# Squares of six RMS norms summed on GpSimd ahead of the ones-product on TensorE

## The chip, the cores and the metric

The kernel runs on one core of a Trainium2 chip. The metric is the device time of one execution in microseconds. The time before is the median of three runs; one further execution was profiled, and all rows are from that one.

## What is computed

The reference is a forward pass over 512 tokens of width 1024 in fp32. It has three layers: an RWKV-7 time mix, an attention layer with low-rank queries and keys (MLA), and a layer with windowed attention beside multiscale pooling. Each is followed by a feed-forward block (width 2816). What matters here is the norm that stands before and behind most of these parts:

```
def rmsnorm(x, g):
    xf = x.astype(jnp.float32)
    y = xf * lax.rsqrt(jnp.mean(xf * xf, axis=-1, keepdims=True) + NORM_EPS)
    return (y * g.astype(jnp.float32)).astype(x.dtype)

x = x + rmsnorm(m, norm_g[layer, 1])                       # behind a mixer's output product
f = conv_ffn(rmsnorm(x, norm_g[layer, 2]), ...)
x = x + rmsnorm(f, norm_g[layer, 3])                       # behind the feed-forward's output product
```

## The kernel before

**Layout.** Activations lie transposed: features on the 128 partitions, the 512 tokens along the free axis, so a width of 1024 is 8 tiles of 128x512 (`x`, `m`). A norm's mean runs over features, thus over partitions and tiles.

**The sum of squares.** For tile j, ScalarE squares a tile into `sq[(first + j) % 2]` (`square`, L559; two buffers in turn). TensorE multiplies the 128x128 constant `ones` with that buffer and adds the result up in PSUM bank 7 over all tiles (`sum_squares`, L1715). This puts the sum over partitions on every partition. ScalarE takes the root into `std` (`root_mean`, L566) and VectorE the reciprocal into `rstd` (L1005). Operands of this product are plain fp32. Each call leaves two records in the trace. The other products here run on operands split in two (`hi` and `lo`, type fp32r).

**Dense stages.** `dense` (L1696) works through units. A unit is one output tile of 128 features by 512 tokens, in bank `r` = unit mod 4. For each of its k tiles it issues three products (`w_hi` with `hi`, `w_lo` with `hi`, `w_hi` with `lo`). `w_o`, `o_w` and `out` have 8 units of 8 k tiles. The last part of each feed-forward's output product (`f0dn2`, `f1dn2`, `f2dn2`) has 8 units of 6 k tiles. With `norm_of` set, the sum of squares j is issued behind unit j + 1, and the last one behind sum 6 at the end of the stage. These six stages feed the norms `n_wo`, `n_f0out`, `n_ow`, `n_f1out`, `n_f2` and `n_final`. The other seven norms (`n_mix`, `n_f0`, `n_mla`, `n_ckv`, `n_cq`, `n_f1`, `n_in`) run elsewhere.

**Weights.** SyncE's queue loads a unit's weights into `w_raw[r]` when its last content has been split. ScalarE copies it rounded into `w_hi[r]` (`high`, L553), VectorE subtracts for `w_lo[r]` (`low`, L999). Both work two units ahead of TensorE (`LEAD = 2`). In ScalarE's queue the copy for unit u + 2 stands before the square of tile u (`over_units`, `square_units`).

**Read-out.** Behind a unit, ScalarE (`w_o`, `o_w`, L774 for `w_o`) or VectorE (L1411 in the `dn` stages, L1664 in `out`) takes the bank to SBUF; the square of that tile follows.

**GpSimd** runs one loop in the RWKV part (L544, masks for the triangular inverse) and nothing afterwards. **gconv** is a 128x512 buffer that the feed-forward's gating uses, and (as `gates[1]`) the gated merge before `out`; no dense stage with a norm behind it uses it.

**Semaphores.** `sq_ready` counts squares, `sq_used` the products of all but a norm's last tile, `sum_ready` the last ones, `std_ready` roots. Square j (from j = 2) waits until product j - 2 has used its buffer.

Of the kernel before, what the change touches and what calls it, by code (L numbers as in the profile page):

```python
# [22 lines left out]
ALU = mybir.AluOpType  # L23
# [117 lines left out]
NORM_AT = {}  # L141
_first = 0
for _i, (_name, _n) in enumerate([("n_mix", 8), ("n_wo", 8), ("n_f0", 8), ("n_f0out", 8), ("n_mla", 8), ("n_ckv", 2),
# [2 lines left out]
    NORM_AT[_name] = (_i, _first, _n)  # L146
    _first += _n

NORMED_AT, _first = {}, 0
for _name, _n in (("f0", 8), ("kv", 8), ("q", 8), ("ckv", 2), ("cq", 3), ("f1", 8), ("in", 8), ("f2", 8)):  # L150
    NORMED_AT[_name] = (_first, _n)
# [3 lines left out]
SCALED_AT, _first = {}, 0  # L155
# [86 lines left out]
def build(nc, dram, out_d):  # L242
    with ExitStack() as ctx:
# [7 lines left out]
        def at(name, shape, offset, dt=F32):  # L251
            return nc.alloc_sbuf_tensor_at(name, list(shape), dt, offset=offset)
# [19 lines left out]
        sq = [at(f"sq{i}", [P, T], SQ0 + ROW * i) for i in range(2)]  # L272
# [6 lines left out]
        G1 = place(ROW)  # L279
        gpad, gconv = at("gpad", [P, T + 2], G0), at("gconv", [P, T], G1)  # L280
        gact = sq

        def const(name, rows=slice(0, P), lo=0, hi=None):
            a, n = CONST[name] if name in CONST else LATE[name]
            return (consts if name in CONST else late)[rows, a + lo:a + (n if hi is None else hi)]
# [81 lines left out]
        bank = [ctx.enter_context(nc.psum_tensor(f"bank{b}", [P, T], F32)) for b in range(8)]  # L367

        def signals(text):
            return [ctx.enter_context(nc.semaphore(n)) for n in text.split()]  # L370
# [3 lines left out]
            for n in ("w_loaded", "w_high", "w_split", "unit_done", "bank_free"))  # L374
        (const_loaded, x_loaded, x_back, sq_ready, sq_used, sum_ready, std_ready, rstd_ready, omu_ready) = signals(
            "const_loaded x_loaded x_back sq_ready sq_used sum_ready std_ready rstd_ready omu_ready")
        (resid_tmp, x_ready, normed_tmp, normed_high, normed_low, h_ready, out_ready, out_stored) = signals(
            "resid_tmp x_ready normed_tmp normed_high normed_low h_ready out_ready out_stored")
        (mix_base, mix_tmp, mix_high, mix_low, zeroed) = signals(
# [155 lines left out]
        def _(pool):  # L535
            for j in range(DT):
                for lv in range(1, LEVELS + 1):
                    for p in range(2):
# [4 lines left out]
                        mask = const("level", lo=lv * HEAD, hi=(lv + 1) * HEAD).unsqueeze(1).broadcast_to([P, TT, HEAD])  # L543
                        pool.tensor_tensor(off[p][:, :, :], ab[p][:, :, :], mask, ALU.mult).then_inc(off_ready, 1)  # L544


        @block.scalar
        def _(act):
# [5 lines left out]

            def square(name, source, j):
                i, first, n = NORM_AT[name]
                if j >= 2:
                    act.wait_ge(sq_used, first - i + j - 1)
                act.activation(sq[(first + j) % 2][:, :], source(j), ACT.Square).then_inc(sq_ready, 1)  # L559

            def root_mean(name):
# [7 lines left out]
            def norm(name, source, ready):  # L569

                for j in range(NORM_AT[name][2]):
                    ready(j)
                    square(name, source, j)
                root_mean(name)
# [7 lines left out]
            def late_norm(name, tag, ready):  # L582

                for j in range(DT):
                    ready(j)
                    gained(tag, j)
                    square(name, lambda j: x[:, j, :], j)
                root_mean(name)

            def square_units(phase, name, source, read=None, tag=None):  # L590

                def body(i, r, c):
                    if read is not None:
                        act.wait_ge(unit_done[r], c + 1)
                        read(i, r).then_inc(bank_free[r], 1)
                    act.wait_ge(bank_free[r], c + 1)
                    square(name, source, SLOTS * i + r)
                    if tag is not None:
                        gained(tag, SLOTS * i + r)
                over_units(act, phase, body, high)  # L600
                root_mean(name)
# [275 lines left out]
            for g in range(8 * PAIRS):  # L877
                i, t = g // 8, g % 8
# [81 lines left out]
            for g in range(STEPS2):  # L960
                j, t = g // 8, g % 8
# [716 lines left out]
        def _(pe):  # L1678
            def dense(name, operand, ready=None, then=None, norm_of=None, norm_in=None, inside=None):

                def body(i, r, c):
                    hi, lo = operand(r)
                    kt = KS[name][r]
                    pe.wait_ge(w_split[r], c + 1)
                    pe.wait_ge(bank_free[r], c)
                    for k in range(kt):
                        if norm_in is not None and isinstance(i, int) and i == 0 and r == 0:
                            sum_squares(norm_in, k)  # L1690
                        if inside is not None and isinstance(i, int) and i == 0:
                            inside(r, k)
                        if ready is not None and (r == 0 or name == "lora"):
                            ready(r, k)
                        for n, (w, a) in enumerate(((w_hi, hi), (w_lo, hi), (w_hi, lo))):
                            mm = pe.matmul(bank[r][:, :], w[r][:, k, :], a[:, k, :],  # L1696
                                           start=(k == 0 and n == 0), stop=(k == kt - 1 and n == 2))
                    mm.then_inc(unit_done[r], 1)
                    if then is not None:
                        then(i, r)  # L1700
                    if norm_of is not None and SLOTS * i + r:
                        sum_squares(norm_of, SLOTS * i + r - 1)
                if norm_of is None:
                    over_units(pe, name, body, peel=int(norm_in is not None or inside is not None))
                else:
                    for u in range(UNITS[name]):
                        body(u // SLOTS, u % SLOTS, START[name][u % SLOTS] + u // SLOTS)
                    sum_squares(norm_of, UNITS[name] - 1)

            def sum_squares(name, j):  # L1710
                i, first, n = NORM_AT[name]
                if i and j == 0:
                    pe.wait_ge(std_ready, i)
                pe.wait_ge(sq_ready, first + j + 1)
                mm = pe.matmul(bank[7][:, :], const("ones"), sq[(first + j) % 2][:, :], start=(j == 0),  # L1715
                               stop=(j == n - 1))
                mm.then_inc(sum_ready if j == n - 1 else sq_used, 1)

            def norm(name):
                for j in range(NORM_AT[name][2]):  # L1720
# [7 lines left out]
            for phase in ("r", "k"):  # L1728
                q, _, src = MIXES[phase]
# [342 lines left out]
            for g in range(8 * PAIRS):  # L2072
                i, t = g // 8, g % 8
# [3 lines left out]
                before = FILL_FIRST + 8 * i + sum(n for at_t, n in FILL_BLOCKS.items() if at_t < t)  # L2077
# [90 lines left out]
            for g in range(STEPS2):  # L2168
                j, t = g // 8, g % 8
# [162 lines left out]
```

## Time and profile before

| | us |
|---|---|
| median of 3 runs | 2396.14 (2391.94 to 2396.9) |
| the profiled execution's own time | 2399.1 |
| its span, first to last instruction | 2397.2 |
| TensorE busy (matmul) | 2229.6 (93%) |
| VectorE busy | 1300.2 (54%) |
| ScalarE busy | 929.4 (39%) |
| GpSimd busy | 60.7 (3%) |
| L1715, sums of squares: 93 calls, 186 records | 104.2 busy |
| mean granted TensorE clock | 0.968 of full |

Busy time is an average over stages with different limits. What an instruction in a dense stage costs is read from the chain of work that ended last. Each of its pieces gives the start, the length and the engine and line of work that nothing else covered. PE is TensorE, DVE VectorE, ACT ScalarE, POOL GpSimd. The clock row gives the granted TensorE clock in tenths of full speed (9 stands for 90% and more).

### The profile page before, as it was taken

The numbers are of one execution on the slowest core, as the hardware profiler recorded it, in microseconds if no ns is written. First come the engines' busy times: TensorE is split into PE (matmuls) and PEld (weight loads), VectorE is DVE, ScalarE is ACT, GpSimd is POOL, SyncE is SP. The second block draws the span as 40 slices with busy tenths as digits, with TensorE's granted clock in tenths as the row PEclk, the third lists the DMA queues.
The fourth block names the chain that finished last, engine by engine and source line by source line (L and its number), as shares of the span: only waits on it lengthen the run. The fifth ranks groups of instructions, "written<-read, shape, count | busy, mean of one in ns | idle before, by whom it ended". The sixth has DMA issues, their size and how long they took to land.

```text
span 2397.2 us, 37444 instructions
## 1 busy us (share of the span) xinstructions
PE 2229.6 (93%) x14890; PEld 1728.5 (72%) x14890; DVE 1300.2 (54%) x1978; ACT 929.4 (39%) x1471; POOL 60.7 (3%) x84
## 2 busy tenths in 40 slices
PE   4989999987899999879998999999799999999997
PEld 2856666675688888646776888887467787888885
DVE  4565776763563645485654645544654544434343
ACT  4563343332442323345654532323334444322222
POOL 0001111110000000000000000000000000000000
PEclk8999999987999999989999999999899999999999
DMA  3310000003133232201111333332120232332321
GB/s 122 97 33 23 14 18 24 6 2 133 44 106 105 88 105 83 76 29 45 40 48 61 94 99 97 97 94 90 49 71 27 71 106 84 100 97 96 101 84 62
DMA packets 53030, 168.89 MB, mean 70 GB/s; under 512 B 6920, under 2 KB 11144, under 8 KB 52768
## 3 DMA queue, kind: packets, MB, share of 16 engines
q1 hardware_dynamic: 52896, 167.00, 21.9%
q8 instruction: 96, 1.57, 0.3%
q14 instruction: 38, 0.31, 0.0%
HBM read 164.88 MB, written 2.10 MB: 70 GB/s over the span
## 4 chain that ended last, share of the span: by engine, by line
PE 83%; DVE 13%; ACT 2%; issue 1%; DMA 0%; SPq 0%; DVEq 0%; ACTq 0%
PE bank L1696 60%; PE bank L2121 2%; PE bank L1715 2%; PE bank L1765 2%; PE bank L2014 2%; PE bank L1848 1%; DVE rstd L1005 1%; PE bank L2051 1%; PE bank L2033 1%; PE bank L1829 1%; PE bank L2131 1%; DVE rw_k_inv L1149 1%; PE bank L1874 1%; DVE x L1023 1%; DVE tmp L1034 1%
## 5 line engine op out<-in xcount | busy, mean ns | idle before, releaser
L1696 PE MATMUL bank<-a_hi,w_hi 128*128 128x512 f32 x1424 | 575.0, 404 | 38.3 <-DVE w_lo L999 20.1
L1696 PE MATMUL bank<-a_hi,w_lo 128*128 128x512 f32 x1424 | 558.6, 392 | 0.0
L1696 PE MATMUL bank<-a_lo,w_hi 128*128 128x512 f32 x1424 | 558.3, 392 | 0.0
L999 DVE TENSOR_TENSOR w_lo<-w_raw,w_hi 128x1024 fp32r<-128x1024 f32 (+3 forms) x322 | 361.5, 1124 | 252.8 <-ACT w_hi L553 246.9
L553 ACT ACTIVATE w_hi<-w_raw 128x1024 fp32r<-128x1024 f32 (+3 forms) x322 | 311.3, 970 | 184.4 <-PE bank L1696 180.5
L1696 PEld LDWEIGHTS bank<-a_hi,w_hi 128*128 128x128 f32 x1424 | 269.8, 189 | 115.8 <-issue 36.9
L1696 PEld LDWEIGHTS bank<-a_hi,w_lo 128*128 128x128 f32 x1424 | 270.2, 190 | 61.4 <-issue 7.7
L1696 PEld LDWEIGHTS bank<-a_lo,w_hi 128*128 128x128 f32 x1424 | 269.9, 190 | 57.3
L1696 PE MATMUL bank<-b_hi,w_hi 128*128 128x512 f32 x640 | 260.1, 406 | 20.8 <-DVE b_lo L1057 20.3
L1696 PE MATMUL bank<-b_hi,w_lo 128*128 128x512 f32 x640 | 251.1, 392 | 0.0
L1696 PE MATMUL bank<-b_lo,w_hi 128*128 128x512 f32 x640 | 250.9, 392 | 0.0
L1696 PEld LDWEIGHTS bank<-b_hi,w_hi 128*128 128x128 f32 x640 | 120.8, 189 | 56.6 <-issue 24.0
L1715 PE MATMUL bank<-sq,consts 128*128 128x512 f32 x186 | 104.2, 660 | 48.3 <-ACT sq L559 48.3
L1696 PEld LDWEIGHTS bank<-b_hi,w_lo 128*128 128x128 f32 x640 | 121.2, 189 | 28.6 <-issue 4.6
L1696 PEld LDWEIGHTS bank<-b_lo,w_hi 128*128 128x128 f32 x640 | 121.1, 189 | 25.7
L801 ACT ACTIVATE b_hi<-tmp 128x512 f32 (+1 forms) x66 | 41.7, 632 | 172.2 <-DVE tmp L1397 172.2
L792 ACT ACTIVATE gconv<-gpad,vecs 128x512 f32<-128x512 f32 x44 | 36.0, 817 | 184.0 <-DVE gpad L1382 184.0
L1715 PEld LDWEIGHTS bank<-sq,consts 128*128 128x128 f32 x186 | 36.3, 207 | 79.7 <-issue 51.2
L1401 DVE TENSOR_TENSOR b_lo<-tmp,b_hi 128x512 f32 (+1 forms) x66 | 45.7, 693 | 57.1 <-ACT b_hi L801 57.1
L1765 PE MATMUL bank<-v_mix,v_raw 128*128 128x512 f32 (+1 forms) x164 | 74.7, 553 | 0.0
L1005 DVE RECIPROCAL rstd<-std 128x512 f32<-128x512 f32 x13 | 43.6, 3353 | 57.0 <-ACT std L566 57.0
L544 POOL TENSOR_TENSOR rw_off<-rw_ab,consts 128x256 f32<-128x256 f32 x80 | 60.5, 770 | 472.6 <-DVE rw_ab L1213 350.4
(308 smaller groups left out, 2945.8 us busy)
## 6 DMA issues: line engine op xcount, KB each, us to landing
w_raw<-in_f0gu SPq DMA_DIRECT2D x44, 512.0 KB, 3.5
w_raw<-in_f1gu SPq DMA_DIRECT2D x44, 512.0 KB, 3.5
w_raw<-in_f2gu SPq DMA_DIRECT2D x44, 512.0 KB, 3.5
w_raw<-in_f0dn SPq DMA_DIRECT2D x16, 512.0 KB, 3.5
w_raw<-in_f1dn SPq DMA_DIRECT2D x16, 512.0 KB, 3.5
w_raw<-in_f2dn SPq DMA_DIRECT2D x16, 512.0 KB, 3.5
w_raw<-in_in SPq DMA_DIRECT2D x10, 512.0 KB, 3.5
w_raw<-in_r SPq DMA_DIRECT2D x8, 512.0 KB, 6.6
```

The lines of the kernel that those rows point to most:

```text
L544: pool.tensor_tensor(off[p][:, :, :], ab[p][:, :, :], mask, ALU.mult).then_inc(off_ready, 1)
L553: act.activation(w_hi[r][:, 0:n, :], raw[r][:, 0:n, :], ACT.Copy).then_inc(w_high[r], 1)
L792: act.activation(gconv[:, :], gpad[:, 2:T + 2], ACT.Identity, scale=column(vecs, base + 2, 4 * ft), bias=column(vecs, base + 3, 4 * ft))\
L801: act.activation(tile(opnd["b"][0], 2 * i + r // 2), tmp[(r // 2) % 2][:, :], ACT.Copy)\
L999: dve.tensor_tensor(w_lo[r][:, 0:n, :], raw[r][:, 0:n, :], w_hi[r][:, 0:n, :].bitcast(F32), ALU.subtract).then_inc(w_split[r], 1)
L1005: dve.reciprocal(rstd[:, :], std[:, :]).then_inc(rstd_ready, 1)
L1401: dve.tensor_tensor(tile(opnd["b"][1], t), tmp[par][:, :], tile(opnd["b"][0], t).bitcast(F32), ALU.subtract).then_inc(bank_free[r], 1)
L1696: mm = pe.matmul(bank[r][:, :], w[r][:, k, :], a[:, k, :], start=(k == 0 and n == 0), stop=(k == kt - 1 and n == 2))
L1715: mm = pe.matmul(bank[7][:, :], const("ones"), sq[(first + j) % 2][:, :], start=(j == 0), stop=(j == n - 1))
L1765: mm = pe.matmul(bank[V_BANK][:, lo:hi], v_raw[q % 2][:, k, :], v_mix[:, k, lo:hi], start=(k == 0 and lo == 0), stop=(k == DT - 1), skip_g ...
L2014: mm = pe.matmul(bank[u % 2][:, :], w[r][:, k, :], a[:, k, :], start=(k == 0 and n == 0), stop=(k == HEAD_TILES[u % 3] - 1 and n == 2))
L2121: mm = pe.matmul(bank[v % 2][:, :], w[r][:, k, :], a[:, k, :], start=(k == 0 and n == 0), stop=(k == KS[name][0] - 1 and n == 2))
```

## The change

A list `SUMMED` names the six norms behind dense stages. For them GpSimd adds the squares of tiles 0 to 5 into `sq_sum` (the buffer `gconv`): five adds of 128x512 per norm, add j as soon as square j is ready and add j - 1 done. TensorE skips j = 0 to 4. At j = 5 it waits for the fifth add and multiplies `ones` with `sq_sum`; tiles 6 and 7 are multiplied as before. Square j waits for GpSimd's add of the tile whose buffer it overwrites, instead of for TensorE's product. The other seven norms work as before, with their count of `sq_used` renumbered.

```diff
+SUMMED = ("n_wo", "n_f0out", "n_ow", "n_f1out", "n_f2", "n_final")
+ON_POOL = 6
+SQ_USED_AT, _first = {}, 0
+for _name, (_, _, _n) in NORM_AT.items():
+    SQ_USED_AT[_name] = _first
+    _first += 0 if _name in SUMMED else _n - 1
...
+        sq_sum = gconv
...
+            for n, name in enumerate(SUMMED):
+                i, first, _ = NORM_AT[name]
+                for j in range(1, ON_POOL):
+                    pool.wait_ge(sq_ready, first + j + 1)
+                    if j > 1:
+                        pool.wait_ge(pool_summed, n * (ON_POOL - 1) + j - 1)
+                    elif n:
+                        pool.wait_ge(sum_ready, NORM_AT[SUMMED[n - 1]][0] + 1)
+                    before = sq[first % 2] if j == 1 else sq_sum
+                    pool.tensor_tensor(sq_sum[:, :], before[:, :], sq[(first + j) % 2][:, :], ALU.add)\
+                        .then_inc(pool_summed, 1)
...
             def square(name, source, j):
                 i, first, n = NORM_AT[name]
-                if j >= 2:
-                    act.wait_ge(sq_used, first - i + j - 1)
+                if j >= 2 and name in SUMMED:
+                    act.wait_ge(pool_summed, SUMMED.index(name) * (ON_POOL - 1) + max(j - 2, 1))
+                elif j >= 2:
+                    act.wait_ge(sq_used, SQ_USED_AT[name] + j - 1)
...
             def sum_squares(name, j):
                 i, first, n = NORM_AT[name]
-                if i and j == 0:
+                j0 = ON_POOL - 1 if name in SUMMED else 0
+                if j < j0:
+                    return
+                if i and j == j0:
                     pe.wait_ge(std_ready, i)
-                pe.wait_ge(sq_ready, first + j + 1)
-                mm = pe.matmul(bank[7][:, :], const("ones"), sq[(first + j) % 2][:, :], start=(j == 0),
-                               stop=(j == n - 1))
-                mm.then_inc(sum_ready if j == n - 1 else sq_used, 1)
+                if name in SUMMED and j == j0:
+                    pe.wait_ge(pool_summed, (SUMMED.index(name) + 1) * (ON_POOL - 1))
+                else:
+                    pe.wait_ge(sq_ready, first + j + 1)
+                source = sq_sum if name in SUMMED and j == j0 else sq[(first + j) % 2]
+                mm = pe.matmul(bank[7][:, :], const("ones"), source[:, :], start=(j == j0), stop=(j == n - 1))
+                if j == n - 1:
+                    mm.then_inc(sum_ready, 1)
+                elif name not in SUMMED:
+                    mm.then_inc(sq_used, 1)
```

## Rows read from the trace of the kernel before

**Rows 1.** The page, parts 1 and 2: busy time by engine, clock in slices.

```profile
PE 2229.6 (93%) x14890; PEld 1728.5 (72%) x14890; DVE 1300.2 (54%) x1978; ACT 929.4 (39%) x1471; POOL 60.7 (3%) x84
PEclk8999999987999999989999999999899999999999
```

**Rows 2.** The page, part 4: the chain that ended last, shares of the span.

```profile
PE 83%; DVE 13%; ACT 2%; issue 1%; DMA 0%; SPq 0%; DVEq 0%; ACTq 0%
PE bank L1696 60%; PE bank L2121 2%; PE bank L1715 2%; PE bank L1765 2%; PE bank L2014 2%; PE bank L1848 1%; DVE rstd L1005 1%; PE bank L2051 1%; PE bank L2033 1%; PE bank L1829 1%; PE bank L2131 1%; DVE rw_k_inv L1149 1%; PE bank L1874 1%; DVE x L1023 1%; DVE tmp L1034 1%
```

**Rows 3.** The chain in order of time: start us, length us, what.

```profile
585.97 5.49 PE bank L1696 x24
...
617.70 5.50 PE bank L1696 x24
...
647.53 329.85 PE bank L1696 x1455
978.24 4.13 PE bank L1696 x18
...
1003.17 4.14 PE bank L1696 x18
```

**Rows 4.** Line L1715: duration in ns, minimum/median/maximum, first and last start.

```profile
L1715 PE MATMUL bank<-sq,consts x186: 590/591/1193, 16.5 to 2384.2; 128*128 128x512 f32 x186
```

**Rows 5.** Timeline of TensorE behind unit 6 of f0dn2: start us, us, what.

```profile
1001.92 0.39 PE L1696 MATMUL bank<-b_lo,w_hi 128*128 128x512 f32 x1
1002.15 1.02 PE L1715 MATMUL bank<-sq,consts 128*128 128x512 f32 x2
1002.61 0.80 PE L1696 MATMUL bank<-b_hi,w_hi 128*128 128x512 f32 x1
1003.25 0.40 PE L1696 MATMUL bank<-b_hi,w_lo 128*128 128x512 f32 x1
```

**Rows 6.** GpSimd's line L544, then its timeline from 299 to 309.

```profile
L544 POOL TENSOR_TENSOR rw_off<-rw_ab,consts x80: 630/638/1562, 187.9 to 532.9; 128x256 f32<-128x256 f32 x80
...
300.26 1.23 POOL L544 TENSOR_TENSOR rw_off<-rw_ab,consts 128x256 f32<-128x256 f32 x2 [3.10 <-PE bank L1829]
306.00 2.15 POOL L544 TENSOR_TENSOR rw_off<-rw_ab,consts 128x256 f32<-128x256 f32 x2 [4.51 <-PE bank L1829]
```

**Rows 7.** Timeline of VectorE beside the second of these.

```profile
305.96 1.16 DVE L1153 TENSOR_TENSOR_SCAN rw_cum<-consts,rw_sig_w 128x512 f32<-128x512 f32 x1
```

**Rows 8.** Timelines of ScalarE and VectorE from unit 5's end in f0dn2.

```profile
998.09 0.63 ACT L559 ACTIVATE sq<-m 128x512 f32<-128x512 f32 x1 [3.62 <-DVE m L1411]
998.62 1.04 ACT L553 ACTIVATE w_hi<-w_raw 128x1024 fp32r<-128x1024 f32 x1
...
997.36 0.69 DVE L1411 TENSOR_TENSOR m<-m,bank 128x512 f32<-128x512 f32 x1 [1.91 <-PE bank L1696]
999.70 1.23 DVE L999 TENSOR_TENSOR w_lo<-w_raw,w_hi 128x1024 fp32r<-128x1024 f32 x1 [1.65 <-ACT w_hi L553]
```

**Rows 9.** Windows: length, busy us (instructions) by engine, clock, DMA share, GB/s.

```profile
core 0: us, PE busy (x) PEld busy (x) DVE busy (x) ACT busy (x) POOL busy (x), PEclk, DMA share, GB/s
650.00:970.00 320.00, 320.00 (x1414) 264.91 (x1413) 173.31 (x209) 109.69 (x131) 0.00 (x0) 1.00 0.30 96
978.20:1003.00 24.80, 24.80 (x102) 18.65 (x100) 8.46 (x10) 6.99 (x10) 0.00 (x0) 1.00 0.28 85
1055.50:1064.00 8.50, 8.50 (x25) 6.82 (x26) 2.46 (x3) 2.58 (x5) 0.00 (x0) 0.66 0.54 185
1065.70:1082.00 16.30, 16.30 (x73) 13.45 (x72) 12.10 (x12) 5.88 (x8) 0.00 (x0) 1.00 0.12 36
```

**Rows 10.** The chain again, behind the ends of w_o and f0dn2.

```profile
634.75 1.28 PE bank L1696 x3
...
1055.49 8.47 PE bank L1696 x24
```

More of the change, by code:

```diff
@@ L376, in build @@
             "const_loaded x_loaded x_back sq_ready sq_used sum_ready std_ready rstd_ready omu_ready")
+        (pool_summed,) = signals("pool_summed")
         (resid_tmp, x_ready, normed_tmp, normed_high, normed_low, h_ready, out_ready, out_stored) = signals(
```

## The prediction

> **What bounds the kernel now.** I read the totals first: TensorE is busy 93% of the span, VectorE 54%, ScalarE 39% and GpSimd 60.7 us in all [rows 1]. Then the chain of work that ended last: 83% of it is TensorE, 60% on the dense products of L1696, and the sums of squares of L1715 are on it with 2% [rows 2]. So whatever leaves TensorE's queue inside a dense stage can shorten the run one for one, unless something else is due at that moment. The third view is the same chain piece by piece. The reader should compare the starts of consecutive units in the stages that the change touches. In `w_o`, units 2 and 7 start at 585.97 and 617.70, five units apart, which is 6.346 us a unit. In `f0dn2` they start at 978.24 and 1003.17, again five units apart, 4.986 us a unit. Without sums the same product goes at 329.85 / 1455 = 0.2267 us [rows 3]. Twenty-four of them (8 k tiles by 3) are 5.441 us and eighteen (6 by 3) 4.081 us. The differences, 0.905 and 0.905 us, are what one ones-product with its surroundings takes from TensorE's stream. The same two paces stand in the chain for `o_w` and `out` (6.35) and for `f1dn2` and `f2dn2` (4.99), and TensorE never stops inside them.
>
> I did not take the price from the duration of a record: all 186 records of L1715 (two for each of 93 calls) have a median of 591 ns [rows 4], but they overlap their neighbours, and 2 x 591 would say 1.18 us. The timeline shows why the pace is better. The sum appears at 1002.15 and the product behind it at 1002.61, with 0.80 us on its record where its neighbours have 0.39 to 0.40 [rows 5]: the two passes, a delay behind them, and a slightly wider spacing of the next few products add up to the 0.905.
>
> **The change part by part.** Removed: in six norms, `sum_squares` returns at once for j = 0 to 4. In each of these stages sum j is issued after unit j + 1, so these five lie behind units 1 to 5, all inside the unbroken stream, at full granted clock (the clock row shows 9 tenths or more through the dense stages [rows 1]). That is 5 x 6 = 30 slots of 0.905 us = 27.2 us, all on the path.
>
> Kept: the products for j = 5 (now with the sum of six squares), 6 and 7, with their cost. The end of each stage, last unit, sum 6, wait for square 7, sum 7, root, reciprocal, has the same steps and the same durations. I cost it at nothing. The wait on `std_ready` moves from j = 0 to j = 5 and was over long ago in both places.
>
> Added: 30 adds of 128x512 on GpSimd, which has nothing else to do after the RWKV tiles [rows 6]. The nearest row is its multiply of 128x256: 638 ns median, 1562 ns at most [rows 6]. Twice these bounds a 128x512 add between 1.28 and 3.12 us; a fixed part in the 638 would push it below 1.28. I take 1.28, because the long one has a visible reason: at 306.00 two multiplies took 2.15 us where two took 1.23 us at 300.26, and a VectorE scan with two SBUF operands ran from 305.96 for 1.16 us [rows 6, 7]. This looks like GpSimd standing still while VectorE reads two SBUF tensors. The Trainium skill (SBUF — State Buffer, Who interferes with whom) states this as a lock: a VectorE instruction with two SBUF inputs and a GpSimd one that reads SBUF exclude one another, and the first to start wins. The trace agrees, with the 0.92 us by which the pair was longer.
>
> Here the VectorE instruction that could collide is the split L999 (`w_raw`, `w_hi`); the read-out L1411 has one input from PSUM. In `f0dn2` square 5 runs from 998.09 to 998.72 and the split starts at 999.70 [rows 8]. The add starts first, at about 998.8, and is over by about 1000.1. If the two exclude one another, the split waits 0.4 us. I cost that at nothing: it serves a unit two further on, at least 4 us later. Were that cover gone, 30 x 0.4 = 12 us would be the most.
>
> The new wait on TensorE: j = 5 waits for the fifth add, with unit 7 and everything else of TensorE queued behind. In `f0dn2` the square ends 1.56 us after unit 5's last product has been issued (read-out from 997.36, square until 998.72 [rows 8]). TensorE comes to the sum one unit later, 4.08 us after about 997.2, at 1001.3. With 1.28 us of add there are 1.2 us to spare, with 3.12 us it is 0.7 us late. That can happen in the three stages of 4.08 us only, since the other three have 1.36 us more: cost 0, at most 3 x 0.7 = 2.1 us.
>
> The new wait on ScalarE: square j waits for add j - 2, and behind it in ScalarE's queue is the copy L553 of the next weights, for which VectorE's split and then TensorE wait. Add j - 2 has a whole unit of at least 4.08 us, less 1.5 us of read-out and square, beyond its own start: cost 0.
>
> What is late next, at the faster pace? Behind a norm-free stretch TensorE is busy 320.00 of 320 us with DMA at a share of 0.30, while VectorE is busy 54% of it, against 34% in the middle of `f0dn2` [rows 9]. So weights arrive at 0.2267 us a product without sums, and the stages here should run at that pace too. No DMA is moved or added, and SyncE's queue is only released earlier.
>
> What the trace can't fix is the clock after the waits. After the norms behind `f0dn2` the granted clock is 0.66 over 1055.5 to 1064, where one `kvd` unit of 24 products takes 8.47 us, and 1.00 in the stretch behind it [rows 9, 10]. At full clock it would be 5.44 us (3.0 less); at half throughout, by the 1.28 us of three products at 634.75, 10.2 us (1.8 more) [rows 10]. Every stage end is moved by 4.5 us, so such stretches may fall otherwise. I put 0 in the sum and -3 to +4 into the range.
>
> **Sum.** The profiled execution took 2399.1 us, 1.9 beyond its span of 2397.2; it lies 3.0 above the median of 2396.14. 2399.1 - 27.2 = 2371.9 for such an execution, and 2396.1 - 27.2 = 2368.9, say 2369, for the median.
>
> **The rivals.**
> The adds come late: an add of 3.12 us, or more, and TensorE waits at j = 5. By the sum above 2.1 us, so 2371; an add of 4 us would be 1.6 us late at three stages and 0.2 us at the others, 5.4 us, so 2374. For it speaks the 1562 ns of one multiply; against it that the add starts before the split.
>
> The faster pace is not reached, because the delayed splits or the loads set it: half of the saving, 2383. Against it speak the paces without sums [rows 3, 9].
>
> The clock after the stage ends decides: at the five stage ends that have work behind them the low stretches lengthen by the 1.8 us of above, 9 us, so 2378, or shorten by as much, 2360.
>
> It does not do what it says, for instance because a slot that leaves only opens a hole in front of the next weights in all six stages: within 0.2% of before, 2396. TensorE's unbroken stream speaks against it.
>
> Slower: GpSimd becomes the pacemaker. ScalarE waits for the add before square j + 2, the weight copy queues behind, TensorE starves. The deciding point is an add longer than the old unit, 4.99 us in three stages and 6.35 us in three. At 8 us the stages would lose 5 x 3 x 3.0 + 5 x 3 x 1.65 = 70 us: 2466. For it speaks only that the trace has no add of this size; against it the 638 ns for half the columns, a quarter of the point of decision. The Trainium skill (GPSIMD Engine Reference, Elementwise — side-by-side cycle accounting) speaks against elementwise work on GpSimd, at 1.96 times VectorE's time for an fp32 add with two inputs; against the 0.69 us of VectorE's 128x512 instruction [rows 8] that would be an estimate of 1.35 us, still far from 4.99.
>
> **How the numbers follow.** Forecast 2369: 0.82. Adds late (2371 to 2374): 0.05. Pace not reached (2383): 0.03. Clock beyond the forecast's own bounds (2360 or 2378): 0.05. No change: 0.02. Slower: 0.03. The range: below, 2369 less 3 for the clock and 3 for the scatter of the medians (the runs of before span 5 us), 2363; above, 2369 plus 4 for the clock and 2 for late adds, 2375. What this kernel's measurement can tell from no change is about 0.2%, 4.8 us. Faster by more than that: 0.82 + 0.05 + 0.03 + 0.05 = 0.95; within: 0.02; slower: 0.03.
>
> **What would show it.** Right: L1715 has 126 records in place of 186; the chain's unit starts are 5.44 us apart in `w_o`, `o_w`, `out` and 4.08 us in the three `dn2` stages up to unit 6; 30 GpSimd adds of 1.2 to 1.4 us; no idle time before TensorE's j = 5 sum that GpSimd released; each stage 4.5 us shorter and the stretches between them unchanged within 1 us. Wrong: adds above 2.4 us, TensorE idle behind L999 inside the six stages, unit starts still above 5.5 or 4.2 us, or stage ends longer by more than the clock explains.

## The result

The changed kernel takes 2375.89 us (median of four executions, 2370.42 to 2377.76) against 2396.52 us. The ratio is 0.9905, with a 95% interval from 0.9885 to 0.9926: 22.8 us less, where I had forecast 27.2 (the plain medians lie 20.6 us apart; from here on I go by the ratios). On a second occasion it was 2374.37 us, ratio 0.9897 (0.9878 to 0.9916), which is 24.7 us less. The median of 2375.89 lies 0.9 us above my range of 2363 to 2375; the ratio, applied to the 2396.14 from which I forecast, gives 2373.4, inside it. The profiled execution of after is one of the faster ones: its own time is 2370.42 us, 28.7 less than that of before. That the profile gives more than 27.2 and the median less is the question of this study.

The page of after, parts 1 and 2, answers to [rows 1]. The time is TensorE's: 26.5 us less busy. GpSimd has 30 instructions more.

```profile
span 2368.5 us, 37383 instructions
PE 2203.1 (93%) x14830; PEld 1717.5 (73%) x14830; DVE 1308.4 (55%) x1978; ACT 929.1 (39%) x1471; POOL 99.4 (4%) x114
PEclk8989999997999999989999999999899999999999
```

The sums of squares in after (line 1745 there; durations in ns: minimum/median/maximum), to compare with [rows 4]: 114 and 12 records, thus 126 in place of 186, with the same 0.59 us each. The 12 read the sum, in `gconv`.

```profile
L1745 PE MATMUL bank<-sq,consts x114: 590/593/1193, 15.8 to 2355.5; 128*128 128x512 f32 x114
L1745 PE MATMUL bank<-gconv,consts x12: 590/591/592, 610.2 to 2348.8; 128*128 128x512 f32 x12
```

GpSimd's adds in after (line 564), to compare with the multiply of [rows 6]: 1.29 us, all 30 within 20 ns.

```profile
L564 POOL TENSOR_TENSOR gconv<-gconv,sq x24: 1287/1292/1305, 589.9 to 2345.9; 128x512 f32<-128x512 f32 x24
L564 POOL TENSOR_TENSOR gconv<-sq,sq x6: 1292/1296/1301, 584.5 to 2329.6; 128x512 f32<-128x512 f32 x6
```

The chain of after, where [rows 3] showed units with a gap between them. In `w_o`, units 0 to 6 are one piece of 168 products, and only unit 7 stands alone behind the product of the sum. The whole of f0's dense work up to unit 6 of `f0dn2` is one piece of 1545 products (350.30 us, 0.2267 us each).

```profile
570.55 39.76 PE bank L1719 x168
611.17 5.50 PE bank L1719 x24
...
640.99 350.30 PE bank L1719 x1545
992.15 4.14 PE bank L1719 x18
```

To see where the time went I take the starts of the 13 reciprocals `rstd` (one at the end of each norm) in each trace, and their differences. The table shows the time from the norm named before to the norm named, worked out from these starts.

| stretch up to | before | after | after, 2nd profile | slots that left |
|---|---|---|---|---|
| n_wo | 599.57 | 593.41 | 592.34 | 5 |
| n_f0 | 21.87 | 21.86 | 21.85 | |
| n_f0out | 362.53 | 358.04 | 358.01 | 5 |
| n_mla | 17.18 | 17.19 | 17.18 | |
| n_ckv | 40.02 | 38.93 | 39.57 | |
| n_cq | 21.63 | 21.64 | 21.62 | |
| **n_ow** | **210.80** | **207.78** | **211.93** | 5 |
| n_f1 | 21.86 | 21.89 | 21.86 | |
| n_f1out | 362.52 | 357.98 | 358.04 | 5 |
| n_in | 17.19 | 17.19 | 17.18 | |
| n_f2 | 319.08 | 314.54 | 314.50 | 5 |
| n_final | 364.67 | 360.12 | 360.13 | 5 |

Four of the six stretches with five slots less are shorter by 4.48 to 4.58 us in both profiles (forecast 4.53). The stretches between them didn't move, but for `n_ckv`, shorter by 1.1 and 0.5 us. `n_wo` holds the RWKV part too, whose low-clock stretches vary: in the kernel with the last four norms alone, where nothing up to `n_wo` is changed, it took 596.89 us, 2.7 less than in before. The odd one is `n_ow`, which holds the attention layer and `o_w`: 3.0 us shorter in one profile and 1.1 us *longer* in the other, of the same kernel. In the first profile the 1.6 us beyond five slots in `n_wo` and the 1.1 in `n_ckv` outweigh the 1.5 missing in `n_ow`; that is how it comes to more than 27.2.

### The profile page after: what moved, and what is told of

It reads as the page before. It is cut to its first block, busy times and chain, and to the rows that moved or that the text cites. A ratio compares the mean times of both kernels' runs of the same rounds, so it can differ in the third digit from the quotient of the medians.

```text
span 2368.5 us, 37383 instructions
## 1 busy us (share of the span) xinstructions
PE 2203.1 (93%) x14830; PEld 1717.5 (73%) x14830; DVE 1308.4 (55%) x1978; ACT 929.1 (39%) x1471; POOL 99.4 (4%) x114
## 4 chain that ended last, share of the span: by engine, by line
PE 83%; DVE 12%; ACT 2%; issue 1%; DMA 0%; SPq 0%; DVEq 0%; ACTq 0%
PE bank L1719 61%; PE bank L2153 2%; PE bank L1797 2%; PE bank L2046 2%; PE bank L1745 2%; PE bank L1880 1%; DVE rstd L1028 1%; PE bank L2083 1%; PE bank L2065 1%; PE bank L1861 1%; PE bank L2163 1%; DVE rw_k_inv L1172 1%; PE bank L1906 1%; DVE tmp L1057 1%; DVE tmp L1074 1%
## 5 line engine op out<-in xcount | busy, mean ns | idle before, releaser
L1022 DVE TENSOR_TENSOR w_lo<-w_raw,w_hi 128x1024 fp32r<-128x1024 f32 (+3 forms) x322 | 369.9, 1150 | 240.9 <-ACT w_hi L574 235.2
L1719 PE MATMUL bank<-b_hi,w_hi 128*128 128x512 f32 x640 | 254.6, 398 | 20.3 <-DVE b_lo L1080 19.7
L1745 PE MATMUL bank<-sq,consts 128*128 128x512 f32 x114 | 68.6, 713 | 47.3 <-ACT sq L582 47.2
L564 POOL TENSOR_TENSOR gconv<-sq,sq 128x512 f32<-128x512 f32 x6 | 7.8, 1296 | 1693.3 <-ACT sq L582 1693.3
L1745 PEld LDWEIGHTS bank<-sq,consts 128*128 128x128 f32 x114 | 23.0, 220 | 76.3 <-issue 51.0
```

The costliest lines, as they stand in the source:

```text
L1022: dve.tensor_tensor(w_lo[r][:, 0:n, :], raw[r][:, 0:n, :], w_hi[r][:, 0:n, :].bitcast(F32), ALU.subtract).then_inc(w_split[r], 1)
L1719: mm = pe.matmul(bank[r][:, :], w[r][:, k, :], a[:, k, :], start=(k == 0 and n == 0), stop=(k == kt - 1 and n == 2))
L1745: mm = pe.matmul(bank[7][:, :], const("ones"), source[:, :], start=(j == j0), stop=(j == n - 1))
```

## Where the clock falls

Windows of the second profile of after, near the end of the attention layer (length, busy us and instructions by engine, granted clock, DMA share, GB/s):

```profile
1212.00:1216.00 4.00, 2.71 (x18) 1.90 (x16) 3.81 (x9) 2.47 (x7) 0.00 (x0) 1.00 0.43 131
1216.00:1220.00 4.00, 3.21 (x22) 3.24 (x23) 2.11 (x6) 2.02 (x6) 0.00 (x0) 0.80 0.01 2
1220.00:1224.00 4.00, 4.00 (x18) 3.71 (x18) 0.58 (x2) 1.35 (x6) 0.00 (x0) 0.50 0.00 0
1224.00:1228.00 4.00, 2.67 (x7) 1.52 (x7) 1.38 (x4) 0.84 (x3) 0.00 (x0) 0.50 0.01 2
1228.00:1232.00 4.00, 4.00 (x16) 3.02 (x14) 1.29 (x4) 1.21 (x4) 0.00 (x0) 0.50 0.01 4
1232.00:1236.00 4.00, 4.00 (x26) 2.95 (x26) 2.42 (x6) 3.16 (x9) 0.00 (x0) 1.00 0.00 0
```

The same place in the first profile of after:

```profile
1216.00:1220.00 4.00, 2.13 (x16) 1.71 (x15) 3.77 (x8) 2.05 (x5) 0.00 (x0) 1.00 0.25 102
1220.00:1224.00 4.00, 4.00 (x36) 3.90 (x34) 1.39 (x6) 2.50 (x8) 0.00 (x0) 1.00 0.00 0
1224.00:1228.00 4.00, 2.58 (x16) 1.85 (x16) 2.09 (x6) 1.54 (x7) 0.00 (x0) 1.00 0.01 2
```

The last column but two is the granted clock. In the last pairs of heads no products of the head weights are left to fill TensorE's waits (the steps of `fill` run out), and TensorE waits 1.9 us at a stretch for ScalarE. In the second profile the clock was granted at 0.50 (1.2 GHz in place of 2.4) from there for some 13.6 us; in the first, with the same work and waits of the same kind, it stayed at 1.00. Summed over windows of 4 us, the clock lost there is worth 6.8 us of full clock, of which 4.2 us (against 207.78) to 5.6 us (against the 206.3 of before less five slots) reach the end of the stage. So a profile of before (210.80) had this stretch at full clock, and one of after had it at half.

The 1.5 us that 207.78 lies above 206.3 have a place too, at the start of the same layer. These are windows some 8 and 12 us behind the reciprocal of `n_cq`, in the first profile of after and then in the second:

```profile
1085.50:1087.50 2.00, 0.00 (x0) 0.00 (x0) 1.25 (x3) 2.00 (x6) 0.00 (x0) 1.00 0.00 0
1089.50:1091.50 2.00, 2.00 (x6) 1.52 (x6) 0.56 (x1) 1.11 (x3) 0.00 (x0) 0.50 0.54 162
```

```profile
1084.50:1086.50 2.00, 0.00 (x0) 0.00 (x0) 1.23 (x3) 2.00 (x6) 0.00 (x0) 1.00 0.00 0
1088.50:1090.50 2.00, 2.00 (x10) 1.50 (x8) 0.56 (x1) 1.60 (x3) 0.00 (x0) 1.00 0.57 164
```

TensorE stands idle in both, and the clock falls behind it in the first alone, for 1.7 us of full clock. Call this the early fall and the one in the last pairs of heads the late one. Over all profiles here and of the experiments below, but that of the sixfold adds, six have the early one (the first of after, the twofold adds, eight tiles, seven tiles twice, seven with the products), three the late one (the second of after, the first two norms alone, no adds), four have neither (before twice, the last four norms alone, after with the products), and none has both. Why they exclude one another isn't known.

## The experiments

All are compared with the kernel before on the same chip.

**Both kernels again, with a clock beside each execution.** No edit.

> The kernel before, run as its own entry so that each of its executions has a granted clock beside its time. Theory A (the scatter of 5 to 7 us between executions is TensorE's granted clock at the stage ends and is the same for both kernels): times of 2392 to 2399 us, each 0.001 of mean clock worth about 2 us, ratio 1.000. Theory B (the low clock came with the change): all executions here at 0.968 or higher, within 2 us of each other.

> The changed kernel again. Theory A: the saving is 27 us at equal clock (span 2370 at 0.968), and with five rounds the ratio is 0.9885 to 0.9900. Theory B (the change costs clock, so that only 21 to 23 of 27 us are kept): ratio 0.9900 to 0.9915, and mean clocks of 0.963 to 0.966 where the kernel before has 0.968.

Measured: 2397.11 us (twelve executions), ratio 0.9993 (0.9980 to 1.0006), and 2374.37 us. Neither theory holds as it stands. Time and mean clock go together in both kernels: 53 executions of before, from this and the later occasions, run from 2391.7 us at 0.970 to 2404.5 at 0.965. But the levels differ: the mean clock is 0.9688 for before (times 2397.3 on average) and 0.9660 for ten executions of after, which run from 2366.1 at 0.969 to 2378.7 at 0.963. Against that 2397.3 the executions of after at 0.969 save 31 us, those at 0.963 and 0.964 save 19 us. None of these outer ones was profiled: the two profiles of after are of executions at 0.968 and 0.967.

**Half of the change, twice.** The list of norms is cut, to the first two in one kernel and to the last four in the other:

```diff
-SUMMED = ("n_wo", "n_f0out", "n_ow", "n_f1out", "n_f2", "n_final")
+SUMMED = ("n_wo", "n_f0out")
+SUMMED = ("n_ow", "n_f1out", "n_f2", "n_final")
```

> The change for n_wo and n_f0out alone (10 of the 30 slots); the other four norms as before. What is tested is where 1.5 to 5.7 us went in the stretch from n_cq to n_ow, which holds the attention layer and o_w. Theory A (that loss comes from moving the attention layer against TensorE's granted clock, which then falls where it didn't before): w_o and f0dn2 give 9.05 us, and the stretch n_cq to n_ow, in which nothing is changed here, is longer than before's 210.8 us by 1.5 us or more in the profile; median 2389 to 2392. Theory B (the loss is made by the adds of n_ow itself): the stretch takes 210.8 us as before, median 2387 to 2388.

> The change for the last four norms (20 slots); everything up to the attention layer is as before. Theory A (moved against the clock): the stretch n_cq to n_ow takes 210.8 - 4.5 = 206.3 us in the profile, all four stages give 4.5 us, 18.1 us in all, ratio 0.9925. Theory B (the adds of n_ow cost it): the stretch takes 207.8 us or more, as in the changed kernel's profile, and 13 to 16 us are saved, ratio 0.9935 to 0.9945.

Measured: the first two alone 2393.8 us, ratio 0.9983 (0.9972 to 0.9995), 4 us of the 9.05, and above the 2389 to 2392 that I had given; the last four alone 2378.26 us, ratio 0.9924 (0.9911 to 0.9937), the full 18.1 us. The chain's `rstd` pieces at `n_cq` and `n_ow`, of before, of the first two and of the last four in this order:

```profile
1089.65 3.36 DVE rstd L1005
1300.45 3.37 DVE rstd L1005
```

```profile
1078.03 3.37 DVE rstd L1028
1294.43 3.37 DVE rstd L1028
```

```profile
1087.13 3.36 DVE rstd L1028
1293.32 3.36 DVE rstd L1028
```

That is 210.80, 216.40 and 206.19 us. In the middle one nothing of this stretch is changed, and it is 5.6 us longer than in before. The windows of that run show why:

```profile
1216.00:1220.00 4.00, 2.13 (x20) 2.02 (x19) 2.99 (x7) 1.88 (x6) 0.00 (x0) 0.99 0.02 5
1220.00:1224.00 4.00, 4.00 (x20) 3.71 (x18) 0.97 (x4) 1.32 (x6) 0.00 (x0) 0.50 0.00 0
```

Its twelve executions go from 2384.97 at 0.970 to 2396.89 at 0.964, four of them at 0.964, a level that none of the 53 of before has. The five of the last four stay between 2377.4 and 2379.6, at 0.968 to 0.971. By the stretches theory A held in both: the adds of `n_ow` cost nothing, and the fall came with the shortening of the first two norms' stages, which starts the attention layer some 11 us sooner. That the moving alone does it is argued: no run delays the layer again with nothing else changed.

**The 30 products gone with nothing in their place.** GpSimd adds nothing; the squares of tiles 0 to 4 of six norms are left out. ScalarE's waits for the adds go too; only square 7 still waits for a product. The diff shows TensorE's part.

```diff
-                    pe.wait_ge(pool_summed, (SUMMED.index(name) + 1) * (ON_POOL - 1))
-                source = sq_sum if name in SUMMED and j == j0 else sq[(first + j) % 2]
+                pe.wait_ge(sq_ready, first + j + 1)
+                source = sq[(first + j) % 2]
```

> The 30 products leave and nothing takes their place: GpSimd adds nothing, TensorE multiplies the squares of tiles 5, 6 and 7 alone, so six norms lack the squares of tiles 0 to 4. This prices the adds and their handing over. Theory A (they are covered): the same stage lengths as the changed kernel within 0.1 us, the split L1022 back from 1.47 to 1.23 us, median 2370 to 2376. Rival (GpSimd's reads cost the other engines or TensorE's wait costs something): 3 us or more below the changed kernel, stages shorter by 0.5 us each.

Measured: 2377.27 us (2365.4 to 2378.44), ratio 0.9905 (0.9886 to 0.9925), the same as with the adds, and the same scatter, 0.963 to 0.969. The stretches are those of after: 358.00, 358.02, 314.49 and 360.13 us. The median is above the 2376 that I gave as the upper end, by the same falls of the clock (`n_ow` took 211.93 us in its profile). The adds are covered whole. What they do to VectorE shows in the split of the weights, first in after, then without the adds (mean ns of one):

```profile
L1022 DVE TENSOR_TENSOR w_lo<-w_raw,w_hi 128x1024 fp32r<-128x1024 f32 (+3 forms) x322 | 369.9, 1150 | 240.9 <-ACT w_hi L574 235.2
```

```profile
L1011 DVE TENSOR_TENSOR w_lo<-w_raw,w_hi 128x1024 fp32r<-128x1024 f32 (+3 forms) x322 | 361.4, 1124 | 244.0 <-ACT w_hi L562 238.2
```

8.5 us over 30 adds are 0.28 us each, and nobody waits for them.

**Each add twice.** One instruction more per tile, into `gpad`, which nobody reads then.

```diff
+FOLD = 2
-                    pool.tensor_tensor(sq_sum[:, :], before[:, :], sq[(first + j) % 2][:, :], ALU.add)\
-                        .then_inc(pool_summed, 1)
+                    for e in range(FOLD):
+                        if n or j > 1 or e:
+                            pool.wait_ge(pool_summed, (n * (ON_POOL - 1) + j - 1) * FOLD + e)
+                        dst = sq_sum[:, :] if e == FOLD - 1 else gpad[:, 2:T + 2]
+                        pool.tensor_tensor(dst, before[:, :], sq[(first + j) % 2][:, :], ALU.add)\
+                            .then_inc(pool_summed, 1)
```

> Each add is done twice, the first into a buffer that nobody reads, so that an add takes 2 x 1.29 and a handing over, some 2.7 us. In the three stages of 4.08 us a unit, TensorE would come to its j = 5 product some 0.2 to 0.3 us too early; in the other three there is still 1.1 us to spare. By the prediction's margins: n_f0out, n_f1out and n_final longer by 0.2 to 0.4 us each, the others unchanged, 1 us in all. Rival (the hand-over is nearer to the edge than the rows say): 3 us or more, with TensorE idle in the 8 k tile stages too.

Measured: 2374.32 us, ratio 0.9908 (0.9893 to 0.9923); TensorE waits for the sum 2.3 us in all, in three places, 1.0 us at the longest, where I expected 0.2 to 0.4. `n_f0out` and `n_f1out` are longer by 1.2 and 1.3 us, `n_final` by 0.4. (`n_f2` is longer by 1.1 too, but TensorE waits for no sum there, and the clock lost in it is 8.5 us against 6.8.) The times say more than the profile: its three executions at 0.969 take 2374.1 to 2375.8 us, where after has 2366.1 and 2366.9 at the same mean clock, some 8 us for which the 2.9 us of these stretches don't account. I have no trace of such an execution. The size was off because the second add isn't 1.29 us. The timelines show it, GpSimd's in `w_o` first, then VectorE's in `out` with the last split of that stage, beside which no add runs:

```profile
585.33 1.29 POOL L567 TENSOR_TENSOR gpad<-gconv,sq 128x512 f32<-128x512 f32 x1 [1.91 <-ACT sq L584]
586.71 2.15 POOL L567 TENSOR_TENSOR gconv<-gconv,sq 128x512 f32<-128x512 f32 x1
```

```profile
1964.61 2.22 DVE L1024 TENSOR_TENSOR w_lo<-w_raw,w_hi 128x1024 fp32r<-128x1024 f32 x1 [2.27 <-ACT w_hi L576]
1986.37 1.23 DVE L1024 TENSOR_TENSOR w_lo<-w_raw,w_hi 128x1024 fp32r<-128x1024 f32 x1 [2.26 <-ACT w_hi L576]
```

The first add holds up the split, which starts meanwhile and shows 2.22 us in place of 1.23. The second add waits in turn for the split and shows 2.15. That is the exclusion of the prediction, in both directions, and it agrees with the lock that the Trainium skill (SBUF — State Buffer, Who interferes with whom) describes.

**Each add six times**, to make the slower rival true on purpose.

```diff
-FOLD = 2
+FOLD = 6
```

> Each add is done six times, five of them into a buffer that nobody reads: 6 x 1.29 us, five handings over and one split of VectorE waited for, about 9.1 us a tile. This makes the prediction's slower rival true on purpose. By that rival's formula (each of five tiles costs what the add exceeds the old unit by): 15 x (9.1 - 4.99) + 15 x (9.1 - 6.35) = 103 us above before, 2499. By a chain of five adds that starts at square 1 and ends at TensorE's j = 5, against the units that run meanwhile (18.9 us in the dn2 stages, 25.7 us in the others): 3 x 26 + 3 x 20 = 138 us above the changed kernel, 2512.

Measured: 2522.02 us (one execution). TensorE's waits in that run (us in total, times, longest):

```profile
PE bank L1747 <- POOL gconv L567: 138.5, 6, 25.7
```

138.5 us, as the chain of five adds says (138). The time is 10 us above the 2512 of that sum. The clock falls to 0.50 within such a wait and is still there when TensorE resumes (the sum at j = 5 in `f0dn2` shows 2.05 us on its records where before's has 1.02), which I take for most of it. The rival's formula in the prediction (each tile costs what it exceeds the unit by) gave 103 us above before and was wrong in form; the measured time lies 125 us above. TensorE waits for GpSimd at j = 5 alone, six times, since ScalarE's copies run two units ahead and keep it fed nearly until then. The path of the rival does show: ScalarE's squares wait for adds 155.1 us in all, and TensorE waits for a split 0.9 us in each of the three `dn2` stages, which it doesn't in after.

**Seven and eight tiles on GpSimd.**

```diff
-ON_POOL = 6
+ON_POOL = 7
```

and the same with 8.

> Seven tiles added up on GpSimd in place of six: one more add per norm, TensorE multiplies the sum and the last tile. The product that leaves is sum 5, a slot inside the stream; sum 6 becomes the product of the sum, behind unit 7, in the time in which TensorE waits for square 7 anyway. Theory of slots: 6 x 0.905 = 5.4 us less than the changed kernel, ratio 0.986 to 0.988. Rival (the end of the stage is already bound by something that this lengthens, the add of tile 6 at 1.29 us coming late): no gain or up to 2 us of loss against the changed kernel.

> All eight tiles added up on GpSimd, one product per norm. In the stream nothing more leaves than with seven. At the stage end the product now waits for square 7 and then for an add of 1.29 us. Theory: 5 to 6 stage ends longer by about 1.3 us (in out the end is partly hidden), so 6 to 8 us more than with seven, about 1 to 3 us more than the changed kernel. Rival (the product of sum 6 was still running when square 7 came, and its leaving pays for the add): same as with seven.

> Seven tiles on GpSimd again, on another occasion: 2396.5 - 27.2 - 5.4 = 2364 if no execution has the fall of the clock in the attention layer; a mean of 2366 to 2368 with executions at 2370 if some have it.

Measured: seven 2364.94 us, ratio 0.9870 (0.9855 to 0.9885), and again 2364.68 us, 0.9866 (0.9850 to 0.9883). It beats the kernel before clearly; against after the intervals still overlap (0.9878 to 0.9885), and it is the stretches that show the gain. The stretches `n_f0out`, `n_f1out` and `n_final` are 0.9 us below after's, one slot each. The nine executions lie between 2362.4 and 2370.8 at clocks of 0.968 to 0.973, and neither of its two profiles has the late fall: of the 9.4 us below after's 2374.37, 5.4 are slots, and the rest I put down to the clock. Eight takes 2375.87 us, ratio 0.9914 (0.9899 to 0.9929), 10.9 us above seven, where I expected 6 to 8. The chain at the end of `f0dn2`, seven first and then eight:

```profile
994.98 0.02 ACT sq L582
995.00 0.62 issue
995.63 1.28 ACT L589
996.92 0.70 ACT std L589
```

```profile
996.93 0.64 ACT sq L582
997.57 0.07 issue
997.64 1.27 POOL gconv L564
998.91 0.14 issue
999.04 1.11 PE bank L1745 x2
1000.18 0.70 ACT std L589
```

With seven, the last product runs beside the load of ScalarE's table (1.28 us) and costs nothing. With eight, the add is in the chain, 1.3 us more at this end. The six stretches are 1.8, 1.3, 2.2, 1.7, 0.9 and 3.7 us longer than seven's. The parts above 1.3 go with granted clock (86.1 us of full clock lost over the run by 4 us windows, against 73.5), which I have not taken apart further.

**Products into the thin pairs.** 20 products that nobody reads, in the last two pairs of heads (in place of the dots stands a wait, once, for the bank that they write):

```diff
+                if (i == PAIRS - 2 and t in (3, 5)) or (i == PAIRS - 1 and t in (1, 3, 5)):
+                    ...
+                    for _ in range(4):
+                        pe.matmul(bank[0][:, :], cq[0][:, 0, 0:P], cq[0][:, 0, :], start=True, stop=True)
```

> The changed kernel with 20 products of 128x512 added for TensorE, in the last two pairs of heads of the attention layer, where no products of the head weights are left to fill its waits. They write a bank that is free and whose content nobody reads. Theory A (the lost part of the saving is TensorE's clock falling in these thin pairs): the stretch n_cq to n_ow is 206.3 us plus at most 2 us of products that find no gap, no granted clock below 1 between 1200 and 1240, executions with clocks of 0.963 to 0.966 gone, median 2369 to 2371. Rival (the clock has nothing to do with the thin pairs, or falls anyway): 20 x 0.227 = 4.5 us slower than the changed kernel, 2378, or the same scatter of 2366 to 2378.

> Seven tiles on GpSimd, with the same 20 products. Theory A: its executions without the fall (all five of the first time) get longer by the 0 to 2 us of products without a gap: 2364 to 2367. If the fall happens here in part of the executions too, the filling wins by its mean: 2363 to 2365 against 2366 of the mean without.

Measured: after with them 2369.21 us (four executions, 2367.49 to 2373.97, clocks 0.967 to 0.970), ratio 0.9895 (0.9877 to 0.9913). In its profile the clock stays at 1.00 there, and `n_ow` takes 207.93 us, 1.6 above the 206.3 of undisturbed work, which is the price of the products (neither the late nor the early fall is there):

```profile
1200.00:1220.00 20.00, 19.24 (x127) 16.25 (x126) 11.72 (x29) 13.65 (x39) 0.00 (x0) 1.00 0.18 54
1220.00:1236.00 16.00, 14.64 (x93) 11.75 (x92) 6.41 (x16) 8.26 (x20) 0.00 (x0) 1.00 0.01 2
```

Theory A expects all of this: work added, time not lost, and the executions at 0.963 to 0.966 (six of ten without) absent. But four executions are few, and the ratio's interval overlaps that of after (0.9878 to 0.9916), so the sign of the whole isn't shown by the times. Seven with them takes 2364.86 us, 0.9869 (0.9852 to 0.9885), the same as seven without: 1.8 us more in `n_ow` by the profiles (208.68 against 206.86), no gain, since it had no fall to prevent.

## Why the prediction was right or wrong

- **The price of a slot**, 0.905 us from the pace of units and not 2 x 591 ns: right. Four stretches gave 4.48 to 4.58 us for five slots; the last four norms alone gave 18.2 us for 20 slots. The prediction explains the 0.905 by two passes, a delay and wider spacing. It is also four times the pace of an fp32r product (4 x 0.2267 = 0.907), which is simpler; no run here tells the two apart.
- **All 30 on the path**: right. With the products gone and no adds, the stretches have the same length as in after.
- **The add at 1.28 us** of a range up to 3.12: right, 1.29, with no fixed part to be seen against 0.638 for half the columns. It started first and VectorE's split was the one to wait, 0.28 us on average where I had 0.4.
- **Margins of the new waits**: right that TensorE never waits at j = 5 in after. The margin of 1.2 us in the `dn2` stages is real (in `f0dn2` the fifth add ends at 989.97 and the product of the sum starts at 991.13), but the doubled adds used it up faster than their number says, because they collide with the split.
- **Stage ends unchanged**: right for the norms' own stretches, 21.9 and 17.2 us throughout. The stretch up to `n_ckv` missed the 1 us that I allowed, by 0.1 in one profile.
- **The clock, 0 in the sum and -3 to +4 in the range**: this step failed. I looked for it only where TensorE was already at half clock in before, behind the stage ends, and priced only those. The place that decided had a clock of 1.00 throughout in the profile of before: the last pairs of heads. The term came out at +4.4 us on the first occasion (22.8 for 27.2) and +2.5 on the second (24.7); the late fall is 5.6 us in the one execution of after whose profile has it. I had the slots right to 0.1 us in four of the six stages, and a median 7 us above my forecast. What the executions at 0.963 and 0.964 lose beyond the late fall is not shown, since none was profiled.
- **The rivals.** Late adds, a pace not reached and no change didn't occur. The clock rival (2378) is nearest to the slower half of after's executions (2375 to 2379); it puts the loss at the stage ends, and the place found is the attention layer, but those executions were not profiled. The slower one could be made true with adds of 9 us, but its formula was wrong.

What stays open is why the clock falls in some executions and not in others of the same kernel. The start of the attention layer doesn't decide it: the late fall was seen with starts (the reciprocal of `n_cq`) at 1076.5, 1078.0 and 1080.2, the early one from 1074.1 to 1078.5, seven's second profile at 1076.6 among them. At 1087 to 1090 neither was seen, in three profiles.

## What to carry to other kernels

Price an instruction in a saturated queue by the pace of the units with and without it, not by its record, and check it by a table of stretches between fixed marks, which separates the term that is right from the one that is not. When a change moves work in time, look for places behind it where TensorE is thinly fed but still at full clock: they can fall to half, and an unchanged stretch then takes back a part of the gain (here 2.5 to 4.4 of 27 us were missing; one profile shows the place). A sum handed to another engine should stop one short of the end: the last tile goes straight to the product, so that the hand-over never stands in the last chain (seven against eight tiles: 11 us, of which six adds of 1.3 us in the chain make 7 to 8).

## What the hardware showed that I had not expected

- The granted clock in one and the same stretch was 1.00 in one profile and 0.50 for some 13.6 us in another, of the same kernel with the same longest waits (207.78 and 211.93 us for the stretch). A shorter fall at the start of the layer was seen only in profiles without this one.
- Adding 20 products went with a median 5 us lower (2369.21 against 2374.37), their own cost of 1.6 to 1.8 us included; the intervals of the ratios overlap.
- GpSimd and VectorE, each with two SBUF operands, take turns by whole instructions: 1.29 us became 2.15 and 1.23 became 2.22.
